# A two-block decoder kernel: the second block's projections, pooling, recurrence and attention put into one stream of 14 weight units, and output product, norm and store into one last stage

## The reference

```python
h = _rmsnorm(x, pre_norm_g[l])
proj = jnp.einsum('btd,de->bte', h, w_in[l])
q_a, f_a, i_a, g_a, u_b, g_b, q_c, k_c, v_c, g_c, f_c = jnp.split(proj, IN_SPLIT_POINTS, axis=-1)
...
o_a = _hgrn2_chunkwise(jax.nn.silu(q_a).reshape(hshape), k_a.reshape(hshape),
...
pooled = _multiscale_pool(u_b)
...
o_c = _forgetting_attention(q_c.reshape(fshape), k_c.reshape(fshape), v_c.reshape(fshape), log_f_c)
o_c = o_c.reshape(B, T, FOX_WIDTH).astype(x.dtype) * jax.nn.silu(g_c)
...
mixed = jnp.concatenate([o_a, o_b, o_c], axis=-1)
y = jnp.einsum('bte,ed->btd', mixed, w_out[l])
x = x + _rmsnorm(y, post_norm_g[l])
```

## Time and profile before

| | us |
|---|---|
| three runs: lowest, median, highest | 2235.26, 2239.9, 2240.41 |
| the profiled execution, its own time | 2236.35 |
| its span, first to last instruction | 2233.2 |
| PE, DVE, ACT, POOL busy | 2051.1, 1065.2, 865.9, 153.7 |

### The profile page before, as it was taken

One profiled execution on the slowest core, in us unless ns is written; L12 is line 12 of the kernel. 1 busy time (PEld: TensorE's weight loads), 2 busy tenths in 40 slices (PEclk: granted clock), 3 DMA queues, 4 the chain that ended last, 5 costly groups with the idle time before them and its releaser, 6 DMA issues. The chain is left out here.

```text
span 2233.2 us, 31464 instructions
## 1 busy us (share of the span) xinstructions
PE 2051.1 (92%) x12820; PEld 1800.9 (81%) x12820; DVE 1065.2 (48%) x1722; ACT 865.9 (39%) x1367; POOL 153.7 (7%) x161
## 2 busy tenths in 40 slices
PE   7999998999698999999899778999999898799795
PEld 7999997898597999999798556888888586666584
DVE  6666675755733333333432663433343555522144
ACT  6557632455723422332232452422333333132231
POOL 0011211122300000000000200000000001000001
PEclk9999996799899999999999999999999999555697
DMA  7223431133341223222231141322222231000111
GB/s 174 77 95 115 136 118 33 45 77 77 91 122 55 97 93 95 94 76 93 58 96 51 36 124 53 98 95 94 94 94 94 60 93 57 1 0 1 38 38 38
DMA packets 202029, 171.78 MB, mean 77 GB/s; under 512 B 41096, under 2 KB 176264, under 8 KB 201912
## 3 DMA queue, kind: packets, MB, share of 16 engines
q1 hardware_dynamic: 201912, 170.14, 25.7%
HBM read 159.30 MB, written 10.82 MB: 76 GB/s over the span
## 5 line engine op out<-in xcount | busy, mean ns | idle before, releaser
L171 PE MATMUL ps<-gdn_xhi,gdnf_whi 128*128 128x264 f32 x768 | 162.8, 294 | 5.2 <-DVE gdn_xlo L502 4.4
L171 PE MATMUL ps<-gdn_xlo,gdnf_whi 128*128 128x264 f32 x768 | 158.6, 288 | 0.0
L171 PE MATMUL ps<-gdn_xhi,gdnf_wlo 128*128 128x264 f32 x768 | 158.3, 288 | 0.0
L348 DVE TENSOR_TENSOR h<-h,ps 128x528 f32<-128x528 f32 (+1 forms) x128 | 87.6, 694 | 146.4 <-PE ps L171 146.4
L149 ACT CAST ffn0w_whi<-raw 128x2048 fp32r<-128x2048 f32 x32 | 61.0, 1905 | 229.7 <-PE ps L171 229.7
L149 ACT CAST ffn1w_whi<-raw 128x2048 fp32r<-128x2048 f32 x32 | 60.9, 1904 | 213.0 <-PE ps L171 213.0
L156 DVE TENSOR_TENSOR ffn0w_wlo<-raw,ffn0w_whi 128x2048 fp32r<-128x2048 f32 x32 | 73.4, 2293 | 145.0 <-ACT ffn0w_whi L149 145.0
L156 DVE TENSOR_TENSOR ffn1w_wlo<-raw,ffn1w_whi 128x2048 fp32r<-128x2048 f32 x32 | 73.4, 2293 | 136.8 <-ACT ffn1w_whi L149 136.8
L171 PEld LDWEIGHTS ps<-gdn_xhi,gdnf_whi 128*128 128x128 f32 x768 | 123.0, 192 | 6.9 <-issue 4.8
L171 PEld LDWEIGHTS ps<-gdn_xlo,gdnf_whi 128*128 128x128 f32 x768 | 121.4, 192 | 0.0
L171 PEld LDWEIGHTS ps<-gdn_xhi,gdnf_wlo 128*128 128x128 f32 x768 | 121.0, 192 | 0.0
(11 more groups left out here) (498 smaller groups left out, 5073.1 us busy)
## 6 DMA issues: line engine op xcount, KB each, us to landing
raw<-in_ff_up_dram SPq DMA_DIRECT2D x32, 1024.0 KB, 5.4
raw<-in_ff_down_dram SPq DMA_DIRECT2D x32, 1024.0 KB, 5.0
raw<-in_gdn_in_dram SPq DMA_DIRECT2D x24, 1024.0 KB, 5.7
raw<-in_w_in_dram SPq DMA_DIRECT2D x14, 1024.0 KB, 5.3
raw<-in_mlstm_in_dram SPq DMA_DIRECT2D x12, 1024.0 KB, 5.3
raw<-in_gdn_out_dram SPq DMA_DIRECT2D x8, 1024.0 KB, 7.2
gdn_v_spilled<-gdnf_o SPq DMA_DIRECT2D x16, 264.0 KB, 2.2
gdn_z_spilled<-gdnf_o SPq DMA_DIRECT2D x16, 264.0 KB, 2.3
```

What stands on the lines that cost most here:

```text
L171: mm = pe.matmul(ps[:, b, 0:k.width], w, x[:, half], start=first and n == 0, stop=last and n == 2)
L348: dve.tensor_tensor(parted(k, acc[:, j, k.now]), parted(k, acc[:, j, k.now]), filled(k, k.ps[j % 4]), ALU.add).then_inc(s.down_free, 1)
```

## The change

`second` now has two stages. The first, `second_mix`, streams 14 units (the 10 of before and the 4 of gate columns, in another order, `SEC_COLS`). The units are counted by u, their tiles by j = 0 to 27. Within a tile there are three places x = 0, 1, 2 (after three, six and eight of the eight feature tiles) where each engine's function `beside(j, x)` puts other work into its own queue. Pooling and the gates of the recurrence and of the attention come at the first tiles, the seven levels at j = 8 to 14, the recurrence's read-out from (15, 1) to (17, 1), and the 32 attention steps, now in two groups of four heads, at every place from j = 17 on. Three units (`BY_TOKEN`) come out with tokens on partitions, with the input as the stationary operand and 256 columns a matmul, which replaces the transposes of the values. The mask of the attention is added on POOL to the gate rows `nb` (32 additions of 128 x 128) instead of by a product on PE, and `nb` is filled by 8 DMAs from DRAM instead of by products and copies. Dense tiles use two PSUM banks where four were used. One of the two reciprocals over 128 x 1024 is gone, by other algebra.

The second stage, `finish`, computes SiLU of the gates, the product with the values and its split, the 8 output tiles, transposes of `h` and of the tiles between them, a sum of squares by POOL additions and a product with one column, and then one multiply-add of 128 x 512 for each half row block, followed by the DMAs to the output.

```diff
+SEC_COLS = (1024, 256, 0, 512, 1536, 2048, 2560, 1792, 2304, 2816, 768, 1280, 3072, 3328)
+SECN = len(SEC_COLS)
+BY_TOKEN = (3, 6, 9)
+LEV0 = 8
+FOX0 = 17
...
+            for i, (g, c, h) in enumerate(fox_steps):
+                if c < NCH - 1:
+                    pool.wait_ge(s.maxed, i - 3)
+                diagonal = nb[:, 4 * g + h, chunk(c)]
+                pool.tensor_tensor(diagonal, diagonal, above[:, :], ALU.add).then_inc(s.above_in, 1)
...
+            def fox(i):
...
+                    act.wait_ge(s.negated, i + 1)
+                    nc.scalar.activation(sc[:, i % 4, 0:n], sc[:, i % 4, 0:n], ACT.Exp, bias=mx[:, i, 1:2],
+                                         accum_out=sm[:, i // 4, h:h + 1]).then_inc(s.probs, 1)
+                if 1 <= i <= nf:
+                    n = CH * (fox_steps[i - 1][1] + 1)
+                    act.wait_ge(s.p_turned, i)
+                    if i >= 3:
+                        act.wait_ge(s.o_ready, i - 2)
+                    nc.scalar.copy(pt[:, (i - 1) % 2, 0:n], turned(i - 1)[:, 0:n]).then_inc(s.p_done, 1)
...
+            def beside(j, x):
+                if (j, x) == (1, 2):
+                    lower_bounds()
+                    pooling.dve(k, dve, s.left)
+                    gates.dve(k, dve, 1)
+                if (j, x) == (3, 2):
+                    forget()
+                if (j, x) == (5, 2):
+                    scans()
+                    exponents(0)
+                    ends()
+                    scale(0)
+                l = j - LEV0 + 1
+                if x == 2 and 1 <= l < LEVELS:
+                    exponents(l)
                     take(l - 1)
...
+                    scale(l)
+                if (j, x) == (LEV0 + 1, 2):
+                    states()
+                if (j, x) == (LEV0 + LEVELS - 1, 2):
+                    take(LEVELS - 1)
...
+            for j, x in hooks:
+                if x == 2 and j % 2 == 1 and j // 2 + 2 < SECN:
+                    split_lo(k, dve, u0 + j // 2 + 2, ring(j // 2 + 2))
+                beside(j, x)
+            for i in rest:
+                fox(i)
...
+                if 1 <= i <= nf:
+                    turn(i - 1)
+                if 2 <= i <= nf + 1:
+                    values(i - 2)
+                if i % 4 == 2 and i >= 6:
+                    outcome((i - 6) // 4)
+            def beside(j, x):
+                if (j, x) == (1, 2):
+                    gates.pe(k, pe)
+                if (j, x) == (5, 2):
+                    pooling.pe(k, pe, bank_b)
+                if (j, x) == (LEV0, 1):
+                    k_turn()
+                if (j, x) == (LEV0 + 1, 1):
+                    state_updates()
+                l = j - LEV0
+                if x == 2 and 0 <= l < LEVELS:
+                    level(l)
+                if (j, x) == (15, 1):
+                    diagonal()
+                if (j, x) in reads:
+                    read(reads[j, x])
...
+                if j >= FOX0:
+                    fox(fox_at(j, x))
...
+            for j in range(2, nj):
+                u, m = j // 2, j % 2
+                pe.wait_ge(k.lo_done, u0 + u + 1)
+                pe.wait_ge(s.left, j - 1)
...
+                if u in BY_TOKEN:
+                    for i in range(2):
+                        t = slice(S0 + CH * (2 * m + i), S0 + CH * (2 * m + i + 1))
+                        for kt_ in range(KD):
+                            for n, (y, w) in enumerate(((k.xhi, whi), (k.xhi, wlo), (k.xlo, whi))):
+                                mm = pe.matmul(dense[m][:, 2 * P * i:2 * P * (i + 1)], y[:, kt_, t], w[:, kt_, :],
+                                               start=kt_ == 0 and n == 0, stop=kt_ == KD - 1 and n == 2)
...
+            for i in rest:
+                fox(i)
...
+def finish(k, gate, value, gain_row, out):
...
+            for kt in range(KD + 1):
+                if kt < KD:
+                    nc.scalar.activation(gate[:, kt, :], gate[:, kt, :], ACT.Silu).then_inc(s.gated, 1)
+                if kt > 0:
+                    act.wait_ge(s.scaled, kt)
+                    nc.scalar.copy(ahi[:, kt - 1, :], a[:, (kt - 1) % 2, :]).then_inc(s.a_hi, 1)
...
+            for j in range(2 * n):
+                dve.wait_ge(k.tile_full, t0 + j + 1)
...
+                dve.tensor_scalar(yg[:, j % 2, :], tile_bank(j), gain[:, j:j + 1], None, ALU.mult).then_inc(s.gained, 1)
...
+                if 1 <= j < 4:
+                    for g in (2 * j, 2 * j + 1):
+                        h_out(g)
+            dve.wait_ge(s.inv, 1)
+            dve.wait_ge(s.y_out, 2 * n)
             for c in range(NCH):
...
+                for x in (slice(0, 512), slice(512, D)):
+                    dve.scalar_tensor_tensor(out=fin[:, c, x], in0=yt[:, c, x], scalar=rinv[:, c:c + 1], in1=ht[:, c, x],
+                                             op0=ALU.mult, op1=ALU.add).then_inc(s.made, 1)
...
+        weight_ring(k, "sec", c)
+        mix, gate = sb("mix", [P, KD, SEQ]), sb("gate", [P, KD, SEQ])
...
+            split_rings(k, "sec", c2)
+            second_mix(k, second_unit(ins), ins["pre_norm_g_2"][0], ins["lower_bounds_2"], ins["hgrn_norm_g_2"][0],
+                       w[:, 3584:3584 + FH], ins["fox_f_bias_2"][0], ins["pool_w_2"][0], ins["pool_scale_2"][0], mix, gate,
+                       [tall(ins["w_out_2"][0], 256 * u) for u in range(4)])
+        finish(k, gate, mix, ins["post_norm_g_2"][0], out)
```

More of the change, by code:

```diff
@@ L571, in _ @@
             store(act, nc.scalar.copy, 1)
[L574 to L616, removed]
 def rounds(eng, n, body, period=2):
@@ L3220, in dve @@
             gate_clear(k, dve, self.s)
-            dve.memset(self.one[:, :], 1.0).then_inc(v, 1)
+            dve.memset(self.one, 1.0).then_inc(v, 1)
         if n == 0:
@@ new lines, in second_mix @@
+        pair = lambda ap, c0: ap[:, c0:c0 + 2 * SEQ].rearrange("p (j s) -> p j s", j=2)
+        e1, inv, small, grown = (pair(early, 2 * SEQ * i) for i in range(4))
+        rows = lambda n, t: (early[:, 0:n * t].rearrange("p (a t) -> p a t", a=n) if n > 1 else early[:, 4 * T:5 * T])
+        pu, pa, pc = (late[:, 2 * T * i:2 * T * (i + 1)].rearrange("p (j t) -> p j t", j=2) for i in range(3))
+        e = late[:, 0:4 * SEQ].rearrange("p (l j s) -> p l j s", l=2, j=2)
+        qd, kd = pair(late, 4 * SEQ), pair(late, 6 * SEQ)
@@ L3412, in _ @@
             norm.sync(k, sp)
+            for u in range(loaded, RAW_SLOTS):
+                load_unit(k, sp, u0 + u, cols(u), ring(u))
+            with nc.allow_non_contiguous_dma(reason="256 bounds and gains, feature on partitions"):
+                sp.dma_start(lx[:, :], lower[0].rearrange("(t p) -> p t", p=P)).then_inc(s.lx_in, 16)
+                sp.dma_start(hgain[:, :], hgrn_gain.rearrange("(t p) -> p t", p=P)).then_inc(s.hgain_in, 16)
+            gates.sync(k, sp)
+            pooling.sync(k, sp)
@@ new lines, in level @@
+            def level(l):
+                hf, bl = 1 << l, 2 << l
+                pe.wait_ge(s.scaled, 2 * l + 2)
+                if l == 0:
+                    pe.wait_ge(pooling.out, 2)
+                if l == 1:
+                    pe.wait_ge(gates.v, 2)
+                if l >= 2:
+                    pe.wait_ge(s.taken, 4 * (l - 1))
+                for i in range(2):
+                    for c in range(NCH):
+                        for o_ in range(2):
+                            v = e[half(o_), l % 2, i, chunk(c)]
+                            mm = pe.matmul(level_bank(l, o_)[:, SEQ // 2 * i + CH // 2 * c:SEQ // 2 * i + CH // 2 * (c + 1)], v,
+                                           v.rearrange("p (b w) -> p b w", w=bl)[:, :, hf:bl], start=True, stop=True)
+                mm.then_inc(s.scores, 1)
@@ L3453, in second @@
+    k.unit += n
+    k.tile += 2 * n
+def second(k, ins, out):
     nc = k.nc
@@ L3533, in STAGES @@
     ffn(k, ins, 1, [second_unit(ins)(u) for u in range(4)])
-    second(k, ins)
-    k.y = k.h
+    second(k, ins, out)
 def build(nc, ins, out):
```

1140 lines of the change are left out of this document (601 added, 539 removed).

## The result

The changed kernel takes 2117.1 us (median of 4 runs, 2113.5 to 2121.2), the kernel before 2240.2 beside it: ratio 0.9454, 95% interval 0.9431 to 0.9477. 2117 was forecast. The total hides errors of opposite sign in the forecast's terms, and they are what is to be learned here.

The account below looks back on a forecast made before the run. Some 206 us of the second block ran at about half clock, some 35 behind the last product. Start 1779.3, work 225.5, waits and clock 31.0, last stage 76.2 gave a 2112.0 span, hence 2117 us; range 2094 to 2150.

Parts of the forecast that it names:

- Rival E: Stream: small products keep the clock down throughout, dense tiles included; slower, all at half clock 2342 us; chance 0.02.
- Unit 4: Stream's start: PE waits 2.0 us for this unit's split, behind the forget gate, reciprocal and nine passes on VectorE.
- Keys' transposes: Stream, before the levels: PE waits 3.4 us for scans, end factors and first exponents.
- pooling as a thin cover: Stream's start: unit 3's split done at 27.3, wanted at 29.8 after pooling's products; no stall, by 2.5 us.
- Levels and attention: Stream: PE waits 6.0 us at four of seven levels and 10.0 at attention's odd tiles' ends over four units.
- The hops' 3.5: Stream: hops of about 0.1 us at some 35 places, 3.5 us in all.
- the end's waits: Stream's end: last attention steps behind tile 27 have no dense work beside them, 2.5 us.
- PE's work: Stream: dense tiles, tiles by token, gate product, pooling's products, HGRN and attention at full clock sum to 225.5 us.
- The clock: Stream: PE may lose the clock in the gap at the transposes of the keys; 3.3 us put in once.
- The last stage: `finish`: 22.3 us to the first output tile, six more tiles with transposes, then the end; 76.2 us.
- B: Rival: the stream idles 20.5% as the mLSTM's does, 283.6 us, total 2141, cases 2127 to 2150; chance 0.25.
- D: Rival: part of the stream at half clock, or `nb` late; 40 to 100 us of work, 2150 to 2229; chance 0.06.

Follow-up runs that it names:

- e1: Changed kernel with all 32 attention steps moved behind tile 27, no dense work beside them; 2150.7 us, ratio 0.9616.
- e9: Changed kernel with the next unit's rounding and split behind the small work at tiles j = 9 to 23, levels' and attention's; 2100.3 us, ratio 0.9389.
- e4: Changed kernel with VectorE's pooling chain left out, two copies of the input in its place; 2115.2 us, ratio 0.9459.
- e2: Changed kernel with the next unit's rounding and split behind the attention step instead of ahead, tiles 17 to 23; 2105.8 us, ratio 0.9420.
- e7: Changed kernel with the attention gate's first operation ahead of pooling on VectorE and ACT's three at (1, 2); 2115.4 us, ratio 0.9462.
- e10: Changed kernel with the edits of e7 and e9 together; 2097.4 us, ratio 0.9370.
- e3: Changed kernel without the 32 causal mask additions on POOL; 2114.6 us, ratio 0.9463.
- e5: Changed kernel with eight products that nobody reads put on PE in the last stage's gap; 2118.6 us, ratio 0.9466.
- e11: Changed kernel with 12 products that nobody reads put on PE in the last stage's gap; 2123.1 us, ratio 0.9474.

## Why the prediction was right, and where it was right by luck

**What binds and why it gets faster.** The forecast rested on HGRN and attention getting the full clock beside dense tiles. For the attention this is shown: e1 takes it alone away, and PE's time for the attention goes from 52.1 to 98.1 us. For HGRN it is read from the traces and was not tried by itself: 47.6 us of PE before, 24.9 now and 23.3 in e9. Over the whole block, 84 of the 117.7 us are clock that PE's busy time got back. Rival E (slower) needed 121 us of full-clock work at half; it was some 17 us of time at half, worth 8.5.

**First splits.** Unit 3 had no wait: its split ended at 1810.5, PE's need is at 1812.9. Unit 4: 1.2, forecast 2.0. Keys' transposes: 2.7, forecast 3.4. Here the walk was right, but its sentence on pooling as a thin cover named the wrong owner: e4 shows that ACT's place (3, 2) covers all but 0.8 us of pooling.

**Levels and attention: too dear.** 3.4 at three places instead of 6.0 at four, and 5.8 instead of 10.0. Places and releasers are those named (exponentials at four odd tiles' ends), and e2 and e9 show the cause, rounding and split ahead of the step, but the terms were 1.7 times what came. The hops' 3.5 don't appear as waits; the end's waits are 1.2, not 2.5.

**PE's work: too cheap.** 235.6 with the dips taken out, and the same in e9 without any, not 225.5. Two thirds of the difference are the changes between dense and small matmuls, 0.16 us at each of 40 places, for which the sum had no term; attention itself is 2.7 over, tiles by token 1.8.

**The clock: too cheap.** 8.5, not 3.3. Four waits of 1.0 to 2.7 us came with half clock; the forecast put in one.

So +10.1 of work at full clock and +5.2 of clock stand against -12.4 of waits, 2.8 in all before rounding. The last stage met its 76.2 nearly term by term: the first two output tiles come 24.4 us behind ACT's last work (22.3 forecast), six tiles with their transposes take 38.9 (39.8), and from the last tile's gain to the end it is 13.3 (14.1). This too has luck in it, since the same code took 73.3 to 76.4 us with the length of its low clock. With the stream's three errors of one sign the result would have lain 28 us off: 2145, still in the range, or 2089, outside it. That 2117 was met to the microsecond is luck.

Two figures of the rivals don't follow from their own terms, and nothing rests on them: B's 27 us more than 2117 is 2144, not 2141, and D's 40 to 100 us of work are 2157 to 2217, not 2150 to 2229.

**What stays open.** Whether a wait drops the clock isn't settled by its length. The wait at the keys' transposes was 2.7 us in the changed kernel (some 3 us of low clock), 2.7 in e9 (none), 1.9 in e7 (10 us), 1.9 in e10 (none); and in the changed kernel itself the longest wait for an exponential, 2.1 us at 1977, had no dip, while that of 1.0 at 2002 had. It isn't the instructions in front either: up to that wait e9 has the order of e2, which had the dip, and e10 that of e7. Yet the four executions with the same stream (the changed kernel, e3, e5, e11) had the same four dips at the same places. What else decides wasn't found. What the change's other parts are worth by themselves (the mask product and the values' transposes gone, the tiles by token, `nb` by DMA) wasn't tried.
